# A hybrid linear-attention block on one core: decay weights made in the projection, loaded in the mixing stage, and idle products in TensorE's waits

## The chip, the cores and the metric

One core of a Trainium2 chip runs the whole program. The metric is the device time of one execution in microseconds (us), the median of several. PE is TensorE's matmul stream, DVE is VectorE, ACT is ScalarE, POOL is GpSimd, and SP is SyncE, which here only issues DMAs.

## What is computed

One layer over 1024 latent tokens and 256 context tokens of width 1024, in float32, then a final norm of the latent tokens. Cut to what matters here:

```python
p = h @ w_in                                   # q_a k_a v_a g_a r_a | qkv_b g_b a_b beta_b
# group A: gated linear attention, 4 heads, dk 64, dv 128; both directions
lr = einsum('btr,zrk->zbtk', r_a, w_lr) + b_lr
log_a = log_sigmoid(lr) / 16                   # decay of every key dimension
b = cumsum(log_a within a chunk)
scores = sum_d q[i] k[j] exp(b[i] - b[j])      # j <= i, inside a chunk
dS = (k * exp(b_last - b))^T v                 # state of a chunk
inter = (q * exp(b)) @ S_prev
# group B: gated delta rule, 4 heads, chunk 64: a triangular system is solved per chunk,
# and the state is carried from chunk to chunk; both directions
x = x + gt1 * (concat(norm(o_a)*silu(g_a), norm(o_b)*silu(g_b)) @ w_out)
x = x + gt2 * (relu(norm(x) @ w1)**2 @ w2)
```

## The kernel before

The program has five phases, each a block of instruction streams, one stream per engine, with semaphores between them: `modulate_phase` (norm and modulation), `project_phase` (the product with `w_in`), `mix_phase` (both attention groups), `merge_phase` (output product) and `mlp_phase`. The order on each engine is written out by hand, and an engine never overtakes a waiting instruction.

**Projection.** Products are made with split operands (high and low part, three matmuls for each), over 15 units of at most 256 columns of `w_in`. Each unit is turned into outputs, which are listed in order in `outs`; the outputs go round robin through three PSUM buffers `ps_main`, so that PE may start output i once ACT has copied output i-3. The last units are `ka`, `qa` (keys and queries of group A), two `va` units with 10 tiles of 128 tokens each, and four `gate` units with 8 tiles each. ACT copies every tile (L817), makes the high part of the next unit's weights at the first output of a unit (`split`, L713), and DVE makes the low part (L849). In the gate units, PE also makes 32 groups of late modulation columns, one behind each tile: it loads 512 KB of `w_ada` for each (SP, L585, four buffers), multiplies (`late_columns`, L981), DVE copies the row (`late_out`, L894), and PE turns the row of the tile before (`late_turn`, L987), for which DVE's copy must be there. The low-rank decay of group A (10 outputs `lr`, one for each token tile) is made among the k and v units: a matmul, then on ACT a copy, Abs, Exp and Ln (L755 and L783 to L787), and one operation on DVE (L947); POOL stores it as the scratch tensor `la`.

**Mixing.** Ten steps: two for the context tiles, then eight for the latent tiles. Step p prepares tile p (PE: `system`, `turn_system`, six `level`s, that double the size of the solved blocks) and carries the delta-rule state over tile r = p-1 (`solve`, `update`, `answer`, `predict`, `query`). Between two levels DVE merges a result into `zz` (`factor`, L1538) and ACT copies its transpose (`keep_turned`, L1415); PE's next level waits for both. Group A's work lies between these: PE sums the decays (`cumulate`, L1800), ACT copies the sums (L1433, L1435) and takes the chunk's rates, DVE makes differences for the keys (`differ_keys`, L1579) and for six levels of block size (`differ_level`, L1588 and L1590, two operations each), ACT takes their exponentials (L1449, L1454, L1445), and POOL multiplies them with keys and queries (L1344, L1349, L1356). PE then makes `scores` in two groups (levels 0 to 2 and 3 to 5), turns the keys, and makes the chunk states and the outputs. The steps 0 to 2 have idle products already (`keep_busy`, L1863), products with the unit matrix whose result nobody reads: 34, 34 and 22 of them.

In ACT's stream of a step, what stands between the copies for level 2 and level 3 is `delta(r, 1)` ahead and then this:

```python
keep_turned(p, 2)
if lat(p):
    decay_level(p, 3)
if p + 1 < NT:
    decay(p + 1)          # 8 Abs and one Exp on the next tile's rows
keep_turned(p, 3)
```

Of the kernel before, what the change touches and what calls it, by code (L numbers as in the profile page):

```python
# [21 lines left out]
ALU = mybir.AluOpType  # L22
# [427 lines left out]
def project_phase(nc, A, K, S):  # L450

    with ExitStack() as ctx:
# [11 lines left out]
        NU = len(UNITS)  # L464
        raw = m.sb("raw", [P, 2, KT, W])
        whi = m.sb("whi", [P, 2, KT, W], F32R)
        wlo = m.sb("wlo", [P, 2, KT, W], F32R)
        u_sb = m.sb("u_sb", [P, NTOK])
        y_sb = m.sb("y_sb", [P, NTOK])
        z_sb = m.sb("z_sb", [P, 2, NTOK])  # L470
        sq_sb = m.sb("sq_sb", [P, NTOK])
        n_sb = m.sb("n_sb", [P, 2, NTOK])
        tok_sb = m.sb("tok_sb", [P, 2, NT, P])
        a_sb = m.sb("a_sb", [P, NTOK])
# [6 lines left out]
        lr_x = m.sb("lr_x", [P, 2, 512])  # L481
# [17 lines left out]
        st_tok, st_a = [m.sem("st_tok0"), m.sem("st_tok1")], m.sem("st_a")  # L499
# [4 lines left out]
        st_lr = [m.sem("st_lr0"), m.sem("st_lr1")]  # L504
# [4 lines left out]
        arow = u_sb[:, :2 * P].rearrange("p (x n) -> p x n", n=P)  # L509
        late = [z_sb[:, 0, :KT * P], z_sb[:, 1, :KT * P], n_sb[:, 0, :KT * P], n_sb[:, 1, :KT * P]]  # L510
        ld_a = [m.sem(f"ld_a{i}") for i in range(4)]
# [5 lines left out]
        VA = [un[0] for un in UNITS].index("va")  # L517
        LAST_GATE = NU - 1
        sum_m = lr_x[:].rearrange("p a n -> p (a n)")[:, :6 * P].rearrange("p (x d n) -> p x d n", x=3, d=2)
        rowt = lr_e[:80, :3 * P]  # L520
# [3 lines left out]
        for u, (kind, _, width, h0) in enumerate(UNITS):  # L524
# [3 lines left out]
            elif kind in ("k", "v", "q", "ka", "qa"):  # L528
                for j in range(2):
                    for s in range(2 if kind in ("q", "qa") else 3):  # L530
                        outs.append((u, kind, j, s))
                        n_lr = sum(o[1] == "lr" for o in outs)
                        if n_lr < NT:
                            outs.append((u, "lr", n_lr, 0))
            else:
                for t in range(TL if kind == "gate" else NT):
                    outs.append((u, kind, t, 0))

# [19 lines left out]

        block = ctx.enter_context(nc.Block())
# [7 lines left out]
        def _(sp):  # L567
# [9 lines left out]
            def load_late(g):  # L577
                if g < 2:
                    sp.wait_ge(n_done, 8)
                elif g < 4:  # L580
                    sp.wait_ge(st_n[g - 2], 4 * 16 + 2 * 16)
                else:
                    sp.wait_ge(ar_ready, g - 3)
                c0 = LATE0 + g * P
                sp.dma_start(late[g % 4].rearrange("p (k n) -> p k n", n=P), av[:, :, c0:c0 + P]).then_inc(ld_a[g % 4], 16)  # L585
# [7 lines left out]
            def load_sums():  # L593
                for b in range(2):
                    sp.wait_ge(st_lr[b], 80)
# [2534 lines left out]
```

## Time and profile before

| | us |
|---|---|
| median of 3 runs | 1661.21 |
| lowest and highest | 1659.8, 1670.68 |
| the profiled execution | 1662.78 |
| its span, first to last instruction | 1661.0 |
| PE busy in the span | 1515.7 (91%) |
| DVE busy | 942.2 (57%) |
| ACT busy | 738.9 (44%) |
| POOL busy | 367.4 (22%) |

The profile is of one execution. A span is the time between the first and the last instruction, and the execution is 1.8 us longer. The modulation lasts until about 62 us, the projection until 506 us, the mixing from 508 to 874 us, the output product until about 1005 us, and the MLP until the end.

### The profile page before, as it was taken

What the parts mean: (1) busy time and instruction counts of PE and PEld (TensorE: products, weight loads), DVE (VectorE), ACT (ScalarE), POOL (GpSimd) and SP (SyncE); (2) the same over time, 40 slices, a digit from 0 to 9 for tenths busy, and PEclk for the clock granted to TensorE, in tenths of its full rate; (3) what the DMA queues carried; (4) which work ended last, traced back from release to release, by engine and by line L of the source; (5) the groups of instructions that cost most, each with busy time, mean ns of one, the idle gap of its engine ahead of it and who ended that gap; (6) DMA issues with size and microseconds to landing.
All of it is one profiled execution on the core that took longest, in us unless ns stands there. A gap on an engine that the chain in (4) does not pass through costs nothing. (4 is left out here: it accounts for less than half of the span.)

```text
span 1661.0 us, 34354 instructions
## 1 busy us (share of the span) xinstructions
PE 1515.7 (91%) x14584; PEld 1283.4 (77%) x14584; DVE 942.2 (57%) x1310; ACT 738.9 (44%) x1303; POOL 367.4 (22%) x315
## 2 busy tenths in 40 slices
PE   7699999999996878777778997899999999999997
PEld 6477887899996867766667886788888878888885
DVE  4344553111101487787777439455555598988875
ACT  6477336211114545565544225455555554333333
POOL 0002111111101255565543105232222200000000
PEclk9699999999998999899999999999999999999999
DMA  9313424245554444544414311244444586454322
GB/s 326 87 58 105 130 83 120 84 151 156 172 162 132 130 129 132 153 134 130 123 35 155 125 64 64 95 140 140 159 157 161 174 319 253 142 186 158 122 89 101
DMA packets 179657, 229.94 MB, mean 138 GB/s; under 512 B 34253, under 2 KB 112465, under 8 KB 179506
## 3 DMA queue, kind: packets, MB, share of 16 engines
q1 hardware_dynamic: 172994, 206.91, 38.8%
q0 software_dynamic: 6512, 20.84, 4.0%
q8 instruction: 116, 1.90, 0.5%
q14 instruction: 35, 0.29, 0.1%
HBM read 165.98 MB, written 61.73 MB: 137 GB/s over the span
## 5 line engine op out<-in xcount | busy, mean ns | idle before, releaser
L87 PE MATMUL fps<-xh_m,w1r_hi 128*128 128x512 f32 x448 | 175.9, 393 | 9.5 <-ACT s L2563 2.9
L89 PE MATMUL fps<-xh_m,w1r_lo 128*128 128x512 f32 x448 | 175.2, 391 | 0.0
L87 PE MATMUL fps<-bh,ah 128*128 128x512 f32 x448 | 174.5, 390 | 0.6 <-DVE acc L2892 0.6
L88 PE MATMUL fps<-xl_m,w1r_hi 128*128 128x512 f32 x448 | 175.0, 391 | 0.0
L89 PE MATMUL fps<-bh,al 128*128 128x512 f32 x448 | 174.4, 389 | 0.0
L88 PE MATMUL fps<-bl,ah 128*128 128x512 f32 x448 | 174.4, 389 | 0.0
L80 PE MATMUL ps_main<-hhi,whi 128*128 128x512 f32 (+1 forms) x336 | 126.6, 377 | 0.0
L2535 ACT ACTIVATE ah<-araw 128x2048 fp32r<-128x2048 f32 x28 | 53.7, 1918 | 163.6 <-PE fps L89 134.3
L81 PE MATMUL ps_main<-hlo,whi 128*128 128x512 f32 (+1 forms) x336 | 123.2, 367 | 0.0
L82 PE MATMUL ps_main<-hhi,wlo 128*128 128x512 f32 (+1 forms) x336 | 123.1, 366 | 0.0
L80 PE MATMUL ps_main<-whi,hhi 128*128 128x256 f32 x416 | 120.2, 289 | 0.0
L81 PE MATMUL ps_main<-wlo,hhi 128*128 128x256 f32 x416 | 117.6, 283 | 0.0
L82 PE MATMUL ps_main<-whi,hlo 128*128 128x256 f32 x416 | 117.4, 282 | 0.0
L87 PEld LDWEIGHTS fps<-xh_m,w1r_hi 128*128 128x128 f32 x448 | 84.6, 189 | 29.6 <-issue 7.1
L87 PEld LDWEIGHTS fps<-bh,ah 128*128 128x128 f32 x448 | 84.1, 188 | 18.8 <-issue 1.4
L89 PEld LDWEIGHTS fps<-xh_m,w1r_lo 128*128 128x128 f32 x448 | 84.5, 189 | 17.6
L88 PEld LDWEIGHTS fps<-xl_m,w1r_hi 128*128 128x128 f32 x448 | 84.5, 189 | 17.5
L89 PEld LDWEIGHTS fps<-bh,al 128*128 128x128 f32 x448 | 84.1, 188 | 17.6
L88 PEld LDWEIGHTS fps<-bl,ah 128*128 128x128 f32 x448 | 84.1, 188 | 17.2
L2737 DVE TENSOR_TENSOR w1r_lo<-w1raw,w1r_hi 128x512 fp32r<-128x512 f32 x96 | 74.7, 779 | 36.8 <-ACT w1r_hi L2526 36.8
L817 ACT ACTIVATE t_sb<-ps_main 128x256 f32<-128x256 f32 x52 | 19.9, 383 | 149.8 <-PE ps_main L82 149.8
L849 DVE TENSOR_TENSOR wlo<-raw,whi 128x2048 fp32r<-128x2048 f32 x14 | 32.1, 2292 | 89.9 <-ACT whi L713 89.9
(326 smaller groups left out, 3524.8 us busy)
## 6 DMA issues: line engine op xcount, KB each, us to landing
s_hid<-hb SPq DMA_DIRECT2D x112, 256.0 KB, 2.3
araw<-s_hid SPq DMA_DIRECT2D x28, 1024.0 KB, 5.9
w1raw<-in_w_ff SPq DMA_DIRECT2D x16, 1024.0 KB, 6.0
w2b<-in_w_ff SPq DMA_DIRECT2D x16, 1024.0 KB, 9.9
raw<-in_w_in SPq DMA_DIRECT2D x14, 1024.0 KB, 5.5
z_sb<-in_w_ada SPq DMA_DIRECT2D x16, 512.0 KB, 4.4
n_sb<-in_w_ada SPq DMA_DIRECT2D x16, 512.0 KB, 4.6
kc<-s_k SPq DMA_DIRECT2D x20, 256.0 KB, 3.3
```

The costliest lines, as they stand in the source:

```text
L80: pe.matmul(out, lhi, rhi, start=start, stop=False)
L81: pe.matmul(out, lhi, rlo, start=False, stop=False)
L82: return pe.matmul(out, llo, rhi, start=False, stop=stop)
L87: pe.matmul(out, lhi, rhi, start=start, stop=False, skip_group_check=True)
L88: pe.matmul(out, lhi, rlo, start=False, stop=False, skip_group_check=True)
L89: return pe.matmul(out, llo, rhi, start=False, stop=stop, skip_group_check=True)
L817: act.activation(t_sb[:, nt % 4], ps_main[:, i % 3, :W], ACT.Silu if kind == "gate" else ACT.Copy).then_inc(main_out, 1)
L849: dve.tensor_tensor(wlo[:, u % 2, :, :w], raw[:, u % 2, :, :w], whi[:, u % 2, :, :w].bitcast(F32), ALU.subtract).then_inc(lo_done, 1)
L2535: act.activation(flat(a_hi[v][:]), flat(araw[n % 2][:]), ACT.Copy).then_inc(a_hi_done, 1)
L2737: dve.tensor_tensor(w1r_lo[:, i], weight(n), w1r_hi[:, i].bitcast(F32), ALU.subtract).then_inc(w_lo, 1)
```

## The change

The exponentials of group A's decay leave the mixing stage. The projection makes them, weighs keys and queries with them, and stores the finished tensors (`kin` for the chunk states, `qin` for the outputs between chunks, `wl` for the six levels, `gqk` for keys and queries). The mixing stage loads them.

In the projection: `lr` is made with the key dimension on the partitions, 12 outputs instead of 10 (8 of 512 tokens and 4 of 256), and these stand among the outputs of `qa`, of the first four `va` tiles and of the last four. DVE writes each with two operations and sums it with scans (`decay_sums`: 16, 8 and 16 scans of 130 elements). Then 17 items follow, each 128x2048 elements (one has half that): DVE makes differences (`weight_sums`), ACT exponentials (`weight_exp`), DVE multiplies (`weigh`), SP stores 1 MB. There are two slots for items; an item's differences wait for the store of the item two before. Items 0 to 8 go with the 20 `va` tiles, one for each two tiles, items 9 to 16 with the first 16 gate tiles. The late modulation columns have three buffers instead of four, and their first loads wait for the eighth item.

In the mixing stage: `cumulate`, `differ_*`, `decay_queries/keys/level` and `weigh_level/keys/queries` go, and SP loads `kin`, `gqk`, and `wl` in two halves. A latent step gets thirteen idle products: five in front of `predict(r, 1)`, five in front of level 3, three behind level 4; in the third step, which has `keep_busy` already, only the last three.

```diff
@@ project_phase
+        ITEMS = [(0, kind) for kind in KINDS] + [(2, KIN)] + [(1, kind) for kind in KINDS]
+        starts = [1 + 2 * i for i in range(9)] + [20 + 2 * i for i in range(8)]
+        SUMS_AT = {place(n): i for i, n in enumerate(starts)}
+        WEIGH_AT = {place(n + 1): i for i, n in enumerate(starts)}
@@ sync
             def load_late(g):
-                if g < 2:
-                    sp.wait_ge(n_done, 8)
-                elif g < 4:
-                    sp.wait_ge(st_n[g - 2], 4 * 16 + 2 * 16)
+                if g < NL:
+                    sp.wait_ge(wt_done, 8 if g < 2 else 9)
+                    sp.wait_ge(st_qk, 16)
                 else:
-                    sp.wait_ge(ar_ready, g - 3)
+                    sp.wait_ge(ar_ready, g - NL + 1)
...
+            def store_item(i):
+                t0, n, kind, w, _, _ = item(i)
+                sp.wait_ge(wt_done, i + 1)
...
+                for z in range(2):
+                    sp.dma_start(dst[:, :, z].rearrange("t p a n -> p t (a n)"), w[:, z]).then_inc(st_w[i % 2], 16)
...
+            for g in range(NL, NLATE):
                 load_late(g)
+                if g % 2 == 0 and 9 <= 7 + g // 2 < len(ITEMS):
+                    store_item(7 + g // 2)
@@ scalar
+            def weight_exp(i):
+                t0, n, kind, w, cs, nc_ = item(i)
+                log_exp()
+                act.wait_ge(df_done, i + 1)
+                if kind < KIN:
+                    act.activation(w, w, ACT.Exp, scale=GLA_DECAY).then_inc(ex_done, 1)
+                    return
...
+                    if (u, j) == (VA + 1, 4):
+                        chunk_rates(0)
+                        chunk_rates(2)
+                    if (u, j) == (VA + 2, 0):
+                        chunk_rates(1)
+                    if (u, j) in SUMS_AT:
+                        weight_exp(SUMS_AT[(u, j)])
@@ vector
+            def decay_sums(part):
...
+                dve.wait_ge(lr_done, (4, 12, 8)[part])
+                for x in range(4 * PART[part][1]):
+                    at = slice(2 * PW * x, 2 * PW * (x + 1))
+                    last = dve.tensor_tensor_scan(cs[:, at], restart[:], cs[:, at], 0.0, ALU.mult, ALU.add)
+                last.then_inc(cs_done, 1)
+            def weight_sums(i):
+                t0, n, kind, w, cs, nc_ = item(i)
+                if i >= 2:
+                    dve.wait_ge(st_w[i % 2], 32 * (i // 2))
...
+                dve.tensor_tensor(view(w, 0, out_), view(cs, z + h, edge), view(cs, z, span), ALU.subtract)
+                dve.tensor_tensor(view(w, h, out_), view(cs, h + 1, span), view(cs, h, edge), ALU.subtract)
+                dve.tensor_tensor(view(w, k, out_), view(cs, h, edge), view(cs, 1, span), ALU.subtract)
+                dve.tensor_tensor(view(w, k + h, out_), view(cs, z + h, span), view(cs, z + h, edge),
+                                  ALU.subtract).then_inc(df_done, 1)
+            def weigh(i):
+                t0, n, kind, w, _, _ = item(i)
+                dve.wait_ge(ex_done, i + 1)
...
+                dve.tensor_tensor(w, w, by, ALU.mult).then_inc(wt_done, 1)
...
+                if (u, j) in WEIGH_AT and kind != "lr":
+                    weigh(WEIGH_AT[(u, j)])
+                if (u, j) in SUMS_AT and kind != "lr":
+                    weight_sums(SUMS_AT[(u, j)])
                 if kind == "gate":
                     late_out((u - NU + 4) * TL + j)
@@ mix_phase, sync
             def linear(s):
-                after(sp, kin_done, s)
+                after(sp, kt_ready, s)
+                sp.dma_start(kin[:], S["kin"][s]).then_inc(ld_kin, 16)
                 if lat(s):
...
+                    sp.dma_start(gqk[:], S["gqk"][n]).then_inc(ld_qk, 16)
+                    sp.dma_start(wl[:, 0:3], S["wl"][n, :, 0:3]).then_inc(ld_wl[0], 16)
+                    after(sp, sc_ready, 2 * n)
+                    sp.dma_start(wl[:, 3:6], S["wl"][n, :, 3:6]).then_inc(ld_wl[1], 16)
@@ mix_phase, tensor
+            def idle_states(s, n):
+                pe.wait_ge(gs_out[1], s)
+                for _ in range(n):
+                    pe.matmul(pg[:, 0, :P], K.ident[:], K.ident[:], start=True, stop=True)
+            def idle_solves(s, n):
+                for d in R2:
+                    pe.wait_ge(st_done[d], 2 * s)
+                for _ in range(n):
+                    pe.matmul(pr[1][:, :P], K.ident[:], K.ident[:], start=True, stop=True)
...
-                    cumulate(p)
                     system(p)
...
                     turn_system(p)
                     if p <= TC:
                         keep_busy(p, 4)
+                    else:
+                        idle_states(p, 5)
                 if r is not None:
                     predict(r, 1)
...
                         scores(p, 0)
                     if p <= TC:
                         keep_busy(p, 6)
+                    else:
+                        idle_solves(p, 5)
                     level(p, 3)
...
                     level(p, 4)
                     if p < TC:
                         keep_busy(p, 6)
+                    else:
+                        idle_solves(p, 3)
                     turn_keys(p)
```

## Rows read from the trace of the kernel before

**Rows 1.** Windows of 40 us: PE, PEld, DVE, ACT, POOL busy; PEclk, DMA share, GB/s
```profile
400.00:440.00 40.00, 40.00 (x444) 36.36 (x444) 5.44 (x12) 6.01 (x12) 5.69 (x11) 1.00 0.66 198
...
680.00:720.00 40.00, 31.37 (x907) 28.28 (x898) 30.22 (x63) 23.89 (x66) 22.80 (x18) 0.91 0.45 132
```

**Rows 2.** Waits of PE, 500 to 880 us: total us, times, longest
```profile
PE pd L1734 <- ACT gdn_gt L1415: 30.8, 13, 4.3
PE pr L1748 <- DVE st L1566: 16.4, 9, 2.0
```

**Rows 3.** Timeline of PE, one latent step: start us, us, group [idle before]
```profile
721.66 1.16 PE L1800 MATMUL pg<-tri,gla 128*128 128x128 f32 x8
...
729.90 1.09 PE L1748 MATMUL pr<-st,kc 128*64 128x128 f32 x16 [2.02 <-DVE st L1566]
...
743.55 1.14 PE L1734 MATMUL pd<-gdn_zz,gdn_gt 64*64 64x64 f32 x32 [4.31 <-ACT gdn_gt L1415]
...
745.47 1.71 PE L1748 MATMUL pr<-st,kc 128*64 128x128 f32 x16
...
749.65 0.93 PE L1834 MATMUL pg<-wl 64*64 64x64 f32 x48 [0.73 <-ACT kin L1458]
...
756.07 1.16 PE L1800 MATMUL pg<-tri,gla 128*128 128x128 f32 x8
```

**Rows 4.** Timeline of PE: starts of steps 3 and 9, counted from 0
```profile
614.38 1.16 PE L1800 MATMUL pg<-tri,gla 128*128 128x128 f32 x8
...
829.02 1.16 PE L1800 MATMUL pg<-tri,gla 128*128 128x128 f32 x8
```

**Rows 5.** Timeline of DVE in the latent step before, 686 to 722 us
```profile
689.89 2.32 DVE L1579 TENSOR_TENSOR kin<-bs 128x512 f32<-128x512 f32 x1
...
692.80 1.27 DVE L1566 TENSOR_TENSOR st<-st,pr 128x512 f32<-128x512 f32 x2
...
698.07 0.42 DVE L1590 TENSOR_TENSOR wl<-bs 128x256 f32<-128x256 f32 x1
...
703.77 1.49 DVE L1590 TENSOR_TENSOR wl<-bs 128x256 f32<-128x256 f32 x1
705.18 0.76 DVE L1538 COPY_PREDICATED gdn_zz<-lev_m,pd 128x256 f32<-128x256 uint32 x2
...
713.67 1.11 DVE L1559 SCALAR_TENSOR_TENSOR rr<-pr,gt,vtn 128x128 f32<-128x128 f32 x4
```

**Rows 6.** Timeline of ACT in the same step
```profile
705.29 0.63 ACT L1454 ACTIVATE wl<-wl 128x512 f32<-128x512 f32 x1 [3.10 <-DVE wl L1590]
705.83 2.00 ACT L1393 ACTIVATE ebc<-ebc,gt 128x64 f32<-128x64 f32 x8
...
708.40 0.64 ACT L1415 ACTIVATE gdn_gt<-pd 128x256 f32<-128x256 f32 x2
```

**Rows 7.** Timeline of PE in a context step: eight matrix instructions of four idle products
```profile
554.73 1.16 PE L1863 MATMUL po<-ident 128*128 128x128 f32 x8
```

**Rows 8.** Timeline of ACT in the projection, `va` and gate tiles
```profile
327.40 0.38 ACT L817 ACTIVATE t_sb<-ps_main 128x256 f32<-128x256 f32 x1 [3.61 <-PE ps_main L82]
327.68 1.90 ACT L713 ACTIVATE whi<-raw 128x2048 fp32r<-128x2048 f32 x1
330.28 0.38 ACT L817 ACTIVATE t_sb<-ps_main 128x256 f32<-128x256 f32 x1 [0.70 <-PE ps_main L82]
...
382.84 1.28 ACT L817 ACT_TABLE_LOAD   x1
```

**Rows 9.** Timeline of DVE in the gate tiles
```profile
387.53 2.29 DVE L849 TENSOR_TENSOR wlo<-raw,whi 128x2048 fp32r<-128x2048 f32 x1 [1.32 <-ACT whi L713]
...
393.40 0.29 DVE L894 COPY u_sb<-ps_sq 128x128 f32<-128x128 f32 x1 [3.38 <-PE ps_sq L981]
397.26 0.29 DVE L894 COPY u_sb<-ps_sq 128x128 f32<-128x128 f32 x1 [3.56 <-PE ps_sq L981]
```

**Rows 10.** Timeline of PE in the k units: the matmul of one `lr` output
```profile
121.93 1.12 PE L1060 MATMUL ps_main<-wlr,raT 17*128 17x512 f32 x2
```

More of the change, by code:

```diff
@@ L508, in project_phase @@
         NLATE = (NADA - LATE0) // P
-        arow = u_sb[:, :2 * P].rearrange("p (x n) -> p x n", n=P)
-        late = [z_sb[:, 0, :KT * P], z_sb[:, 1, :KT * P], n_sb[:, 0, :KT * P], n_sb[:, 1, :KT * P]]
-        ld_a = [m.sem(f"ld_a{i}") for i in range(4)]
+        arow = lr_x[:, :2 * P].rearrange("p (x n) -> p x n", n=P)
+        late = [room[:, x:x + KT * P] for x in (0, KT * P, 4 * KT * P)]
+        NL = len(late)
+        ld_a = [m.sem(f"ld_a{i}") for i in range(NL)]
         ar_ready, ar_out, sel_done = m.sem("ar_ready"), m.sem("ar_out"), m.sem("sel_done")
@@ L557, in project_phase, with place, item, view @@
         TURNS = ((0, 4), (4, 4), (8, 2))
+        PART = ((0, 4), (4, 4), (8, 2))
+        KIN, QIN = LEVELS, LEVELS + 1
+        KINDS = [KIN, QIN] + list(range(LEVELS))
+        ITEMS = [(0, kind) for kind in KINDS] + [(2, KIN)] + [(1, kind) for kind in KINDS]
+        def place(n):
+            if n < 2 * NT:
+                return VA + n // NT, n % NT
+            return VA + 2 + (n - 2 * NT) // TL, (n - 2 * NT) % TL
+        starts = [1 + 2 * i for i in range(9)] + [20 + 2 * i for i in range(8)]
+        SUMS_AT = {place(n): i for i, n in enumerate(starts)}
+        WEIGH_AT = {place(n + 1): i for i, n in enumerate(starts)}
+        def item(i):
+            part, kind = ITEMS[i]
+            t0, n = PART[part]
+            return t0, n, kind, slots[i % 2][:, :512 * n], (cs_ctx if part == 2 else cs_lat), 4 * n
+        def view(t, off, dims):
+            return bass.AP(t.tensor, t.offset + off, [t.ap[0]] + dims)
         block = ctx.enter_context(nc.Block())
@@ L621, in _ @@
                 sp.wait_ge(st_g[i], 32)
+            for i in range(2):
+                sp.wait_ge(st_w[i], 32 * ((len(ITEMS) + 1 - i) // 2))
         @block.gpsimd
@@ L1791, in answer @@
                     last.then_inc(o_ready, 1)
-            def cumulate(s):
-                pe.wait_ge(ld_la, 16 * (s + 1))
-                pe.wait_ge(ld_tri, 16)
-                after(pe, gs_out[1], s)
-                for z in R2:
-                    for a in R2:
-                        x = 2 * z + a
-                        last = pe.matmul(pg[:, 0, head(x)], gla[:, head(x)], tri[:, z], start=True, stop=True)
-                last.then_inc(b_ready, 1)
             def turn_keys(s):
-                pe.wait_ge(kin_done, s + 1)
+                pe.wait_ge(ld_kin, 16 * (s + 1))
                 after(pe, gs_out[0], s)
@@ L1868, in step @@
                 if p is not None:
-                    cumulate(p)
                     system(p)
```

368 lines of the change are left out of this document (154 added, 214 removed).

## The prediction, made before the changed kernel was run

> **What bounds the kernel now.** I read the windows first, then PE's waits, then the timelines of one latent step and of the projection's tail. In the gate tiles PE is busy for all 40 us of a window, while DVE works for 5.4 and ACT for 6.0 us of it [rows 1]: the projection is bound by PE, and the two others have room. In the mixing stage PE is busy for 31 of 40 us at a mean granted clock of 0.91, and DVE for 30 [rows 1]: there PE waits in its order for the others. The waits say for what: 30.8 us for the ACT copy L1415 and 16.4 us for DVE's state sum L1566 [rows 2]. In one latent step of 34.4 us (756.07 less 721.66) PE waits 2.02 us ahead of `predict(r, 1)` and 4.31 us ahead of level 3, and twice more for less than 0.8 us each [rows 3]. After the long wait the next groups run slower: 1.14 us for level 3's first half, and 1.71 for a group of `predict` that took 1.09 us earlier in the step [rows 3]. Over steps 3 to 8 a step lasts (829.02 - 614.38) / 6 = 35.8 us [rows 4].
>
> What stands behind the two waits is the work that the change takes away. The state sum at 692.80 starts behind DVE's key difference of 2.32 us [rows 5]. Ahead of level 3, DVE makes the differences of level 3 at 1.49 us for an operation that takes 0.42 us when POOL doesn't multiply, and merges `zz` only at 705.18 [rows 5]; ACT takes an exponential at 705.29, then the 2.0 us of Abs and its Exp, and copies at 708.40 [rows 6].
>
> **Mixing stage, a latent step.** I take the step's queues and set them up again without the removed work, with the durations of the rows. PE's own work: 34.4 less the waits (2.0 + 4.3 + 0.7 + 0.8) and less 1.4 lost at the low clock behind the long wait is 25.2; `cumulate` takes 1.1 of it [rows 3], which leaves 24.1. Thirteen idle products add 13 x 0.235 = 3.1 us, since four of them take 0.94 (eight matrix instructions in 1.16 us, of which about 0.2 overlaps the next group) [rows 7].
> - Ahead of `predict(r, 1)`: DVE's state sum no longer queues behind the key difference and ends some 5.6 us into the step, while PE ends `turn_system` at 6.2. The wait of 2.0 is gone, and the five products that stand in it cost 1.2 us in full.
> - Ahead of level 3: DVE can merge as soon as level 2 is out; ACT makes the Abs and Exp of `decay(p + 1)`, 2.6 us, already while PE is at level 2, and copies right behind the merge. The wait of 4.3 falls to 0.6, and five products fill it: they cost 0.6, and the slow 1.4 us are not lost again.
> - Behind level 4: nothing waited there; three products cost 0.7. Ahead of level 4 a wait of 0.5 is new, because DVE sums the first scores in between (late next on DVE). The waits of 0.7 and 0.8 for ACT's copies of PSUM stay.
> - Sum: 24.1 + 3.1 + 0.5 + 0.7 + 0.8 = 29.2; I take 29.5 us for what the rows don't show. The loads move nothing on the path in this sum: SP issues `kin` and `wl` behind `turn_keys` and the scores, over 15 us ahead of their readers; a step adds 1.3 MB net, 45 GB/s to the 132 that fill 0.45 of the DMA engines [rows 1], which makes about 0.70 in the shorter step. Behind them in SP's queue stand the rows, keys and values of the next tile. If all of this were late, a step would keep some 2.5 us more: 32. If the products cost nothing it would be 28.
> - Six steps save 6 x (35.8 - 29.5) = 38. The last latent step has no long wait and saves 2.7. Step 2 keeps its 22 busy products and saves 4, the context steps lose `cumulate` and a wait behind it, 2 to 2.5 each. Together 49 us, between 36 and 58.
>
> **Projection.** PE's own work hardly changes: 5120 columns of `lr` before and after, at 1.1 us for 512 [rows 10]. New is what DVE and ACT do ahead of PE's releases. An item is a serial chain. DVE's differences of a level are four operations of 512 elements: from 0.42 us for 256 and 2.29 us for 2048 elements [rows 5, 9] about 0.6 us each, 2.4. ACT's exponential of 2048 elements 1.9 (as L713 [rows 8]). DVE's product 2.3 (as L849 [rows 9]). With three handovers of 0.1: 6.9 us, and 5.9 for the items of keys and queries. They can't overlap: DVE's order is product i, then differences i+1, and ACT waits in the middle with PE's next copies queued behind. Two `va` tiles take PE 2 x 2.88 = 5.8 us (330.28 less 327.40 [rows 8]); two gate tiles 7.7 (397.26 less 393.40, doubled [rows 9]). So the chain is slower than PE in the `va` units and just fits the gates.
>
> Going tile by tile from the end of the last `qa` product: the first item starts only at 13 us, behind 16 scans, the unit's low part (2.3) and an `lr`. No row shows a scan; a DVE operation of 128 elements takes 1.11 / 4 = 0.28 [rows 5], and I take 0.35 for 130 (between 0.28 and 0.55): 16 take 5.6. The nine items take 56 us, and within the chain fall the `lr` work of ACT (four operations of 0.4 to 0.6 us each, eight times), eight more scans, and two splits. PE's first gate tile ends at 86 us, where it ended at 62. Of these 24 us, 8 are `lr` products that the k and v units no longer have. That leaves 16 us. Then the last 16 scans come right behind the last `lr`: ACT's rates and item 9 wait for them, and `late_out(0)` stands behind item 9 on DVE. PE waits for it in `late_turn(0)`, 6 us, and in `late_turn(1)`, 5 us, since the unit's split and item 9's product come before `late_out(1)`. The same meeting of split and item at the ninth gate tile costs 2.5. Table loads of 1.28 us [rows 8], two for each item in the gates, lie beside DVE's differences. Waits of 5 us leave PE slow behind them, as in the mixing stage: 2. DMA in the gates: 0.66 of the engines at 198 GB/s [rows 1] is 300 GB/s for all of them, so a 1 MB store needs 3.5 us; 0.66 x 7.7 + 3.5 = 8.6 us of engine time falls into 7.7. With three buffers for the late columns this costs between 0 and 7 us in eight pairs; I take 2. Sum: 16 + 11 + 2.5 + 2 + 2 = 33.5 us, between 15 and 55.
>
> The Trainium skill, "DVE: opcode table, instruction layouts, handler registers and perf-mode slots", section 6, says that the built-in scan runs at half throughput. No row here has a scan. By that rule 130 elements, that stream in about 0.14 us by the slope of rows 5 and 9, would take as much again, the 40 scans 5.5 us longer, of which some 4.5 would reach PE: 1650 instead of 1646.
>
> **Sum.** 1662.8 (the profiled execution) - 49 + 33.5 = 1647.3; that execution is 1.6 us above the median, so 1646 for the median, 0.9% below 1661.2.
>
> **Rivals.**
> 1. The stores hold DVE: slower. An item's differences wait for the store of the item two before, and `late_out` and the splits stand behind that wait on DVE. It decides once a store, queued in SP behind a late load or a unit's weights, lands later than about 4.6 us after the product (7.7 + 6.9 - 10 us that lie between). For it: 8.6 us of DMA work in 7.7, and one queue for both. Against it: the DMA engines are free in the `va` units, and two slots give slack. Each of the eight items of the gates would lose the 3.5 us of one store, and PE some 0.7 at the low clock behind such a wait (half of the 1.4 above): 8 x 4.2 = 34, so 1646 + 34 = 1680.
> 2. DVE and ACT keep up: the projection loses 8 us only. For it: both are idle for more than 80% there [rows 1]. Against it: the chain of 6.9 us in 5.8. 1661.2 - 49 + 8 = 1620.
> 3. The mixing step stays at 32 us: loads or the products take the place of the waits. For it: the rows and the transposed keys are issued late in a step already, and now stand behind 1.5 MB. Then 15 us of the gain go: 1661.
> 4. The idle products do not do what they say: they stand in waits that are gone. This is in the forecast already, as 1.2 + 0.6 + 0.7 = 2.5 us of each of seven steps, 17 us; it has no other time, and only a step without them would tell.
>
> **How the numbers follow.** A measurement of this kernel can tell about 1% from no change, so faster means below 1644.6 and slower above 1677.8. The forecast has 0.45, its own range 1632 to 1660, a bit under half of it below 1644.6. Rival 1 has 0.17, rival 2 0.18, rival 3 0.20. Faster: rival 2, and the lower part of the forecast with a mixing step of 28 us or short waits in the projection, 0.26: 0.44. Slower: rival 1 but for its lower edge, and a little of rival 3 with long scans: 0.16. Same: what is left, 0.40. The range 1616 to 1680 leaves out half of rival 1 and the outer third of rival 2, 0.15.
>
> **What would show it.** In the windows of the `va` and gate tiles PE's busy time falls below 40, with waits of PE for ACT's copies of the `va` tiles and for `late_out`; these two waits should sum to 25 to 35 us, and DVE should be busy above 25 of 40 us. The mixing stage should begin some 33 us later than at 508. Its latent steps should be 29 to 30 us apart, the wait for L1415 ahead of level 3 gone, the clock at 1.00 through most of it, and POOL nearly idle. Wrong would be: steps above 31 us, a projection that ends before 520 us or after 560, or PE waiting for `ld_wl` or `ld_kin`.

## The result, and the profile after

The changed kernel takes 1676.3 us in the median of 14 executions (1663.4 to 1683.4), the kernel before beside it 1661.7 (14 executions). The ratio is 1.0075, with a 95% interval of 1.0061 to 1.009: about 12 us slower (the two medians lie 15 apart), inside the predicted range, but slower where faster was forecast, and 30 us above the predicted 1646. The profiled execution took 1670.2 us (span 1668.4), 6 below its median; I compare it with the profiled 1662.8 of before, so the profiles show only 7 us of the loss.

Three marks divide the program: the last copy of a gate tile (projection's end), the first issue of `kc<-s_k` (mixing's start) and ACT's table load ahead of the output product (mixing's end).

| us | before | after | difference |
|---|---|---|---|
| last gate copy | 504.5 | 533.6 | +29.1 (predicted +33.5) |
| mixing, start to end | 508.4 to 874.0 = 365.6 | 537.3 to 881.4 = 344.1 | -21.5 (predicted -49) |
| rest of the span | 787.0 | 787.0 | 0 |

The first windows answer to [rows 1]. The columns are PE, PEld, DVE, ACT and POOL busy, granted clock, DMA share, GB/s.

```profile
360.00:400.00 40.00, 34.49 (x226) 30.34 (x225) 23.29 (x32) 22.56 (x39) 5.75 (x11) 0.87 0.73 221
400.00:440.00 40.00, 32.48 (x293) 29.64 (x292) 24.38 (x37) 22.51 (x24) 4.15 (x8) 0.83 0.71 222
...
640.00:680.00 40.00, 33.95 (x835) 30.61 (x832) 18.87 (x47) 14.93 (x43) 10.74 (x9) 0.83 0.51 156
680.00:720.00 40.00, 36.31 (x1069) 33.03 (x1071) 22.09 (x55) 18.50 (x55) 13.51 (x11) 1.00 0.63 181
720.00:760.00 40.00, 31.20 (x938) 28.03 (x934) 19.96 (x49) 18.86 (x56) 12.79 (x10) 1.00 0.68 198
```

In the gates PE now idles 7.5 of 40 us, at a mean clock of 0.83. In the mixing stage DVE fell from 30.2 to 22.1 us and POOL from 22.8 to 13.5, as meant; but PE is busy for only 31.2 us of the last window. Apart from one wait for DVE at the start of the stage (8.4 us, until 551) it hardly waits for the two, as PE's waits from 535 to 900 us show (total, times, longest):

```profile
PE pg L1834 <- issue: 10.0, 11, 2.3
PE pd L1733 <- DVE gdn_gt L1565: 8.4, 1, 8.4
PE pg L1856 <- ACT ga_st L1518: 6.1, 8, 0.8
PE pd L1749 <- issue: 5.4, 3, 3.2
PE pd L1745 <- ACT gdn_gt L1498: 3.4, 7, 1.1
...
PE po L1771 <- issue: 2.8, 1, 2.8
PE pd L1745 <- issue: 2.7, 4, 1.4
```

The 30.8 and 16.4 us of [rows 2] are gone: ACT's copy ahead of a level now costs 3.4 us in all, the state sum nothing. In their place stand waits for "issue", for nothing that the profile shows. PE's timeline shows where they fall:

```profile
722.57 0.56 PE L1745 MATMUL pd<-gdn_zz,gdn_gt 64*64 64x64 f32 x21
724.51 0.39 PE L1745 MATMUL pd<-gdn_zz,gdn_gt 64*64 64x64 f32 x10 [1.38 <-issue]
...
727.90 0.60 PE L1874 MATMUL pr<-ident 128*128 128x128 f32 x3
730.49 0.49 PE L1874 MATMUL pr<-ident 128*128 128x128 f32 x3 [2.00 <-issue]
...
828.61 0.37 PE L1749 MATMUL pd<-gdn_gt,gdn_zz 64*64 64x64 f32 x2 [3.15 <-issue]
```

They stand in the middle of a group of like products, even in the middle of idle products that depend on nothing. No semaphore can explain that. So I numbered PE's instructions in the trace by their start (products, weight loads and PE's 640 instructions that only wait), 30,032 of them, and set them beside the packets of the DMA queue that the profile calls "instruction": 117 packets, 1.92 MB, 16,384 bytes each. 1.92 MB over 30,032 instructions is 64 bytes each, so a packet is 256 instructions. From 600 to 870 us PE has eleven gaps above 0.8 us, and all eleven lie at a number that is 193 modulo 256: at the first instruction of such a block. Five successive blocks, worked out from the trace (us):

```
PE enters the    packet of this   its first      idle
block before     block starts     instruction    ahead of it
719.70           721.94           724.51         1.38
724.51           728.10           730.49         2.00
730.49           734.65           736.84         1.26
736.84           739.17           743.25         0
743.25           743.22           748.20         0
```

A block's packet starts only once PE works on the block before it, between 0 and 5.5 us after its entry, and its first instruction runs at the earliest 2.2 us after the packet's start. If PE is through with the block before by then, it stands. From 540 to 870 us the gaps at block borders sum to 4.1 us in the kernel before and to 22.6 us after. I call them code gaps. Of the 11 waits ahead of `scores` (L1834) three are code gaps; the other eight, 0.73 us each, lie anywhere in a block. The kernel before has eight of 0.73 us there too, four of them under the name of ACT's copy [rows 3], so they are something else.

The latent steps, by the first product of `solve(r, 0)`:

```profile
672.47 1.94 PE L1783 MATMUL pr<-rr,gdn_tt 64*64 64x128 f32 x16
...
703.28 1.07 PE L1783 MATMUL pr<-rr,gdn_tt 64*64 64x128 f32 x16
...
738.98 1.07 PE L1783 MATMUL pr<-rr,gdn_tt 64*64 64x128 f32 x16
...
770.90 1.07 PE L1783 MATMUL pr<-rr,gdn_tt 64*64 64x128 f32 x16
```

They lie 30.8, 35.7 and 31.9 us apart, 33.3 on average over seven steps from 634.9 to 868.0, where [rows 4] gave 35.8 and I forecast 29.5. The group at 672.47 took 1.94 us instead of 1.07: behind a code gap of 2.8 us at 666 PE was at the low clock (0.50 from 666 to 673 us).

### The profile page after: what moved, and what is told of

Same layout as the page of the kernel before. It is cut to its first block and busy times, and to the rows that moved or that the text cites. A ratio compares the mean times of both kernels' runs of the same rounds, so it can differ in the third digit from the quotient of the medians.

```text
span 1668.4 us, 34384 instructions
## 1 busy us (share of the span) xinstructions
PE 1536.9 (92%) x14696; PEld 1303.1 (78%) x14696; DVE 945.7 (57%) x1330; ACT 744.8 (45%) x1249; POOL 271.0 (16%) x237
## 3 DMA queue, kind: packets, MB, share of 16 engines
q8 instruction: 117, 1.92, 0.5%
## 5 line engine op out<-in xcount | busy, mean ns | idle before, releaser
L80 PE MATMUL ps_main<-whi,hhi 128*128 128x256 f32 x416 | 127.0, 305 | 6.7 <-ACT t_sb L879 4.2
L81 PE MATMUL ps_main<-wlo,hhi 128*128 128x256 f32 x416 | 123.3, 296 | 0.0
L82 PE MATMUL ps_main<-whi,hlo 128*128 128x256 f32 x416 | 123.2, 296 | 0.0
L87 PEld LDWEIGHTS fps<-xh_m,w1r_hi 128*128 128x128 f32 x448 | 84.5, 189 | 29.6 <-issue 7.4
L80 PEld LDWEIGHTS ps_main<-whi,hhi 128*128 128x128 f32 x416 | 85.2, 205 | 11.8 <-issue 11.8
L82 PEld LDWEIGHTS ps_main<-whi,hlo 128*128 128x128 f32 x416 | 85.5, 205 | 0.0
```

The lines of the kernel that those rows point to most:

```text
L80: pe.matmul(out, lhi, rhi, start=start, stop=False)
L81: pe.matmul(out, lhi, rlo, start=False, stop=False)
L82: return pe.matmul(out, llo, rhi, start=False, stop=stop)
L87: pe.matmul(out, lhi, rhi, start=start, stop=False, skip_group_check=True)
```

## The experiments

Fourteen kernels. "Code gaps" are the sums from 540 to 870 us. Ratios are to the kernel before; mixing is measured by the marks above.

| run | ratio, 95% | last gate copy | mixing | code gaps |
|---|---|---|---|---|
| before | 1 | 504.5 | 365.6 | 4.1 |
| after | 1.0075, 1.0061 to 1.009 | 533.6 | 344.1 | 22.6 |
| e1_no_idle | 1.0001, 0.9973 to 1.0028 | 535.1 | 337.4 | 27.8 |
| e2_wl_once | 1.0077, 1.0047 to 1.0108 | 538.2 | 338.8 | 20.7 |
| e3_halves | 1.006, 1.0032 to 1.0088 | 528.3 | 346.1 | 22.5 |
| e4_before_idle | 1.0005, 0.9985 to 1.0025 | 504.5 | 363.2 | 10.8 |
| e5_no_store | 1.0052, 1.0029 to 1.0075 | 533.2 | 347.6 | 25.9 |
| e6_no_items | 0.9956, 0.9931 to 0.9981 | 517.8 | 341.2 | 24.9 |
| e7_thin | 0.99, 0.9884 to 0.9916 | 534.5 | 318.3 | 6.5 |
| e8_halves_no_idle | 0.9966, 0.9946 to 0.9986 | 531.9 | 331.4 | 24.0 |
| e9_thin_keys | 0.9985, 0.9962 to 1.0009 | 535.5 | 332.7 | 15.8 |
| e10_late_first | 0.9934, 0.9907 to 0.9962 | 529.9 | 334.7 | 26.4 |
| e11_one_place | 0.9968, 0.9941 to 0.9995 | 535.8 | 332.6 | 23.5 |
| e12_paced | 1.047, 1.0443 to 1.0497 | 529.8 | 417.0 | 7.4 |
| e13_before_thin | 0.9994, 0.9975 to 1.0014 | 503.7 | 364.7 | 0 |
| e14_thin_no_idle | 0.9794, 0.9763 to 0.9825 | 535.6 | 298.5 | 6.0 |

Six of these kernels have the projection exactly as changed (after, e1, e2, e7, e9, e14); its end lies at 533.6 to 538.2 there, so one profile tells that mark to about 4 us only. Mixing spreads as much: with the same products and bytes the stage takes 344.1, 346.1 and 347.6 us in after, e3 and e5, and 337.4, 331.4 and 334.7 us in e1, e8 and e10. Differences of 5 us between two single profiles are not clear of that.

**Who holds up PE's code?** First the new loads of the weights alone:

```diff
+                    if n == 0:
-                    sp.dma_start(wl[:, 0:3], ...).then_inc(ld_wl[0], 16)
+                        sp.dma_start(wl[:, 0:3], ...).then_inc(ld_wl[0], 16)
```

and likewise for `wl[:, 3:6]`.

> The changed kernel with the six levels' weights loaded for the first latent step only; later steps take the same ones, so their scores are not the reference's. Theory A, the loads of 1.5 MB in a step hold up the fetches of PE's code: the waits for nothing (in this trace 24 us of PE's waits between 535 and 900 us) fall to the 7 us that the kernel before has, latent steps come to 29.5 us each, and the kernel is about 20 us faster than the changed one, ratio to the kernel before 0.995. Theory B, the loads are innocent: gaps and steps of 33.3 us on average stay, ratio 1.007.

Measured: code gaps of 20.7 us, mixing 5 us shorter, ratio unchanged (1.0077 against 1.0075). Theory A, my first, falls in this form: taking away the weights' 1.5 MB alone gives nothing that can be told from the spread. Then all loads of the stage, by their size:

```diff
+            def thin(s, c=None):
+                if c is None:
+                    return slice(0, 4 if s >= 4 else P)
+                return slice(c * C, c * C + (4 if s >= 4 else C))
-                    sp.dma_start(kc[b][:, d], S["k"][pos(d, s)]).then_inc(ld_kc[b], 16)
+                    sp.dma_start(kc[b][T, d], S["k"][pos(d, s)][T]).then_inc(ld_kc[b], 16)
...
```

> The changed kernel with all loads of the mixing stage but the output weights' cut to four partitions (or four of each half) from the third latent tile's on, so 1/32 or 1/16 of the bytes; the rest of each tile keeps older values, so the result is not the reference's. In the traces so far every wait of PE for nothing of more than 0.8 us falls on a multiple of 256 of PE's own instructions (offset 193), where the next 16 KB of its code begin; the packet starts on average 2.1 us after PE has entered the block before, and 1.8 us or less where the DMA engines are idle. Theory A, the packets start late because the engines are busy with loads: the mean delay falls below 1 us, the waits at block borders from 22.6 us to under 6, a latent step comes to 29.5 us and the kernel is 20 us faster than the changed one, ratio 0.995. Theory B, the fetch is late by itself (one block ahead, PE faster than it): delay and waits stay above 1.6 and 15 us, ratio 1.004 or more.

Theory A, and further than it said in the ratio (0.990, not 0.995). The kernel is 1.7% faster than the changed one, code gaps fall to 6.5 us, and the mixing stage lasts 318.3 us, 47.3 less than before. Windows and two `solve` groups, five steps apart, of this run:

```profile
640.00:680.00 40.00, 37.98 (x1098) 34.69 (x1098) 23.97 (x59) 17.87 (x53) 15.29 (x12) 1.00 0.20 58
680.00:720.00 40.00, 37.18 (x1166) 33.63 (x1159) 24.07 (x61) 23.36 (x70) 12.76 (x10) 1.00 0.08 25
720.00:760.00 40.00, 37.11 (x1013) 33.63 (x1009) 25.08 (x60) 18.25 (x51) 14.63 (x11) 1.00 0.13 37
```

```profile
665.21 1.07 PE L1790 MATMUL pr<-rr,gdn_tt 64*64 64x128 f32 x16
...
812.97 1.07 PE L1790 MATMUL pr<-rr,gdn_tt 64*64 64x128 f32 x16
```

A step is (812.97 - 665.21) / 5 = 29.6 us, and the clock is 1.00 in every window from 600 to 840 us, where after has 0.96, 0.83, 1.00, 1.00, 1.00 and 0.91. That makes the sum of the 26 us that mixing gains here: 16 us of code gaps, and by an estimate 1.4 + 5.8 + 3.0 = 10 us of PE's busy time at the low clock (35.6 x 0.04, 33.95 x 0.17, 33.05 x 0.09). The windows of the whole stage, first the changed kernel's, then this one's, give the same:

```profile
537.30:881.40 344.10, 290.60 (x7672) 261.57 (x7673) 167.85 (x413) 147.02 (x421) 96.30 (x78) 0.95 0.54 161
538.20:856.50 318.30, 280.26 (x7672) 252.78 (x7672) 168.01 (x413) 146.44 (x420) 96.22 (x77) 0.98 0.26 74
```

PE is busy for 10.3 us less with the same products and idle for 15.5 us less. DVE, ACT and POOL are busy for the same times within 0.6 us, so it is not their work that the loads slowed. The clock records of the changed kernel, behind the first 20 us of the stage, have the low level in four stretches, from 627.1, 654.4, 664.6 and 828.5 us on, 24 us in all; each begins in a code gap or less than 1.5 us behind one. The thin run has none there.

Two numbers of the expectation missed: the gaps at block borders were to fall under 6 us (6.5), and the mean delay from PE's entry into the block before to the packet's start fell from 2.1 to 1.45 us only, not below 1.

Only the keys, queries, values and token-major keys cut down (the same edit on four of the loads):

> The changed kernel with only the loads of the old kind cut down that come in packets of 2 KB for both directions' keys, queries, values and token-major keys (2 MB of the some 5.8 MB of a latent step; four partitions of each, or of each half, from the third latent tile's on; the result is not the reference's). The row broadcasts and the weights' loads stay. Theory A, what holds up the fetches of PE's code is the bursts of these loads, that the kernel before has too, and the weights' 1.5 MB only share in it (5 us of 26 by the run that loaded them once): waits at the block borders fall from 22.6 to 12 us or less, the mixing stage from 344 to 330 us or less, ratio 1.000 or less. Theory B, it takes all the traffic together, no one part of it matters: mixing stays above 338 us, ratio 1.005.

Code gaps fall by 7 us, mixing by 11, the ratio by 0.009 (15 us). Between the theories: the old loads alone do about half of what all together do (0.0175, 29 us), the weights alone nothing that shows. What the row broadcasts do by themselves was not run. Over eight changed kernels (after, e1 to e3, e5 to e8), from 600 to 870 us, blocks whose packet came over 2.5 us late had some 127 of the 2 KB packets started in the 1.5 us behind PE's entry, blocks under 1.2 us had some 35; for the 256 byte packets of the row broadcasts it is about 4 against 110. That is a correlation only.

Can the loads be kept and the queues short? On e8:

```diff
                 sp.dma_start(kc[b][:, d], ...).then_inc(ld_kc[b], 16)
+                sp.wait_ge(ld_kc[b], 32 * (s // 2 + 1))
```

and the same behind seven other loads.

> The kernel with halves and without idle products, with the mixing stage's loads paced: SP issues the next group only when the one before has landed (values, keys, queries, query decays, token keys, each 512 KB; gqk 256 KB; the weights 768 KB twice). The same bytes, no burst of more than 768 KB in flight. Theory A, fetches of PE's code are held up by what stands in the DMA queues ahead of them, and short queues let them through: the mean delay falls from 2.0 to 1.5 us, the waits at block borders from 24 to under 15, mixing from 331 us to 322, ratio 0.991. Theory B, the share of busy engines decides, not the queue's length: waits of 20 us or more stay. Theory C, the loads come late for their readers, PE waits for keys or weights: ratio above 1.000.

Theory C, far stronger than thought: 1743 us. The loads come late for their readers, steps of 40 us and more. The waits of all engines, 560 to 940 us:

```profile
ACT ktn L1512 <- DMA ktn<-s_kt: 67.4, 8, 9.8
POOL bbc L1451 <- DMA bbc<-s_row: 56.6, 9, 15.1
```

Its code gaps are small, but a PE that waits up to 9.6 us at a time for ACT gives the fetch its time; it says nothing on the queues.

The control, the same cut in the kernel before:

> The kernel before with its mixing loads cut down as in the thin run of the changed kernel (four partitions, or four of each half, from the third latent tile's on; all but the output weights'; the result is not the reference's). Theory A, the loads hold up PE's code only where nothing else holds PE: before, the waits for ACT and DVE leave the fetch its time (4.1 us of waits at block borders), so the same cut gives at most 5 us here, against 26 in the changed kernel: ratio 0.997 to 1.000. Theory B, the cut itself makes everything faster (shorter waits for loads, less traffic at the engines), and what it gave the changed kernel says nothing of its change: 15 us or more here too, ratio 0.991 or less.

Theory A: 0.9994, and the code gaps go from 4.1 us to none. Its DMA share fell from 0.45 to 0.13, and its waits stayed:

```profile
PE pd L1741 <- ACT gdn_gt L1422: 33.9, 11, 4.3
PE pr L1755 <- DVE st L1573: 16.4, 9, 2.0
```

So less traffic is worth at most 4 us (by the interval) to a PE that waits for ACT and DVE, and 26 us to one that doesn't.

**What do the idle products cost?** They were taken out of the changed kernel:

```diff
-                    else:
-                        idle_solves(p, 5)
...
```

> The changed kernel without the thirteen idle products of a latent step (nothing of the result depends on them). Theory A, the waits of PE for nothing that the profile shows (about 20 us over the mixing stage) are fetches of PE's code held up by the loads of the weights: the gaps stay, a latent step loses only the 2.5 us that the products add, and the kernel is about 15 us faster than the changed one, a ratio to the kernel before of 0.999. Theory B, the gaps come from the products themselves (more instructions to fetch): the gaps go too, steps of 28 us, 30 to 40 us faster, ratio 0.985. Theory C, the products keep the clock up and are worth their time: PE's clock in the latent steps falls below 0.95, steps get no shorter, ratio 1.007 or above.

Theory A, whose 0.999 lies in the interval: 12 us faster (1.0075 - 1.0001; 7 to 17 by the two intervals). One sign of theory C came too, the clock below 0.95. A window:

```profile
720.00:760.00 40.00, 32.69 (x945) 29.40 (x944) 21.75 (x55) 18.98 (x56) 12.46 (x10) 0.88 0.66 195
```

The clock falls, and the code gaps are no fewer (27.8 us). So the products do hold the clock (0.88 here, 1.00 with them; 0.91 and 0.95 over the whole stage), but cost more than it gives. Without loads in the way:

> The changed kernel with the thin loads and without the thirteen idle products (not the reference's result). Theory A, the products cost their 2.5 us in each of seven steps also where the fetches are in time: 12 to 17 us under the thin run's 1646, ratio 0.980 to 0.983, steps of 27 to 28 us. Theory B, without loads in the way the clock that they keep is worth as much as they take: within 4 us of the thin run, ratio 0.988 to 0.992.

Theory A, at or just past the edge of its numbers: 17.6 us under the thin run by the ratios (0.99 - 0.9794), two steps of 26.7 us below (742.41 less 689.00, halved) and 27.3 on average over seven, and the clock stays at 1.00 from 640 to 840 us without one of the thirteen. PE's timeline, then a window:

```profile
689.00 1.07 PE L1790 MATMUL pr<-rr,gdn_tt 64*64 64x128 f32 x16
...
715.79 1.07 PE L1790 MATMUL pr<-rr,gdn_tt 64*64 64x128 f32 x16
...
742.41 1.07 PE L1790 MATMUL pr<-rr,gdn_tt 64*64 64x128 f32 x16
```

```profile
720.00:760.00 40.00, 37.03 (x1223) 33.50 (x1223) 26.12 (x63) 21.78 (x67) 17.17 (x14) 1.00 0.10 26
```

In the kernel before, where the waits still are:

> The kernel before, with the thirteen idle products of a latent step added at the same three places and nothing else. Theory A, they cost what they take where PE doesn't wait and fill the waits of 2.0 and 4.3 us where it does, so that PE is fast behind them: 3.1 us of products a step, of which some 2 lie in waits, and 1.4 us of slow groups saved: within 1 us a step, ratio 0.998 to 1.004. Theory B, the clock is what holds a step at 35.8 us: 1.5 us or more a step gained, ratio 0.993 or less. Theory C, they are pure cost: 3 us in each of seven steps, ratio 1.012.

Theory A: 1.0005. 22 us of PE's two waits are filled (to 18.0 and 7.2 us), mixing is 2.4 us shorter in the profile, and the code gaps grow from 4.1 to 10.8 us. It fits that a PE which runs more meets more often a block that isn't there; no run shows that alone.

> The kernel with halves, and of the thirteen idle products of a latent step only the five ahead of level 3. Their cost by this case's traces is 0.6 to 1.2 us a step (seven steps, 4 to 8 us), what they can give back is the clock (0.87 to 0.91 from 720 us on without any, 0.91 to 1.00 with all). Theory A, cost and clock cancel: ratio 0.995 to 0.998, as without any. Theory B, the clock is worth more than these five: 0.994 or less. Theory C, they only cost: 1.000.

0.9968 against 0.9966 without any: theory A, cost and clock cancel.

**What does the projection lose?** In two halves:

```diff
+                    for z in range(2):
+                        act.wait_ge(df_done, parts(i) + z + 1)
+                        wz = w[:, C * nc_ * z:C * nc_ * (z + 1)]
+                        act.activation(wz, wz, ACT.Exp, scale=GLA_DECAY).then_inc(ex_done, 1)
```

DVE signals behind each pair of its four differences, and multiplies in two operations.

> The changed kernel, with an item of a level made in two halves (one direction each): ACT takes the exponential of the first half while DVE makes the differences of the second, and DVE multiplies the first half while ACT works on the second. The arithmetic and its bytes are the same. Theory A, the serial chain of differences, exponential and product (6.7 us for two va tiles of 5.8 us) is what the projection loses: the chain falls to about 5 us, six items of the va units save about 1.5 us each, the last gate tile ends 8 to 12 us earlier than at 533.6 us. Theory B, the loss lies with the stores and the late columns' three buffers: the projection's end stays within 2 us of 533.6.

In the changed kernel DVE's item in the `va` units looks like this; sums, exponential (ACT, 1.92 us) and product follow each other, and items start 6.7 us apart where nothing else comes between:

```profile
347.32 0.68 DVE L1024 TENSOR_TENSOR room<-room 128x512 f32<-128x512 f32 x1
...
349.13 0.68 DVE L1027 TENSOR_TENSOR room<-room 128x512 f32<-128x512 f32 x1
351.79 2.29 DVE L1038 TENSOR_TENSOR room<-room 128x2048 f32<-128x2048 f32 x1 [1.98 <-ACT room L801]
354.00 0.69 DVE L1024 TENSOR_TENSOR room<-room 128x512 f32<-128x512 f32 x1
```

In halves the wait is gone and they start 4.8 us apart at best:

```profile
350.71 0.67 DVE L1031 TENSOR_TENSOR room<-room 128x512 f32<-128x512 f32 x1
...
354.32 1.22 DVE L1048 TENSOR_TENSOR room<-room 128x1024 f32<-128x1024 f32 x1
355.52 0.69 DVE L1031 TENSOR_TENSOR room<-room 128x512 f32<-128x512 f32 x1
```

But the projection's end moves by 5 us in this profile and by 4 on the mean of four kernels in halves (531.5) against six without (535.4), half of what theory A asked for. The ratios, 1.006 and 1.0075, don't tell the two apart. DVE's timeline shows one reason: an item's differences wait for the store of the item two before, once in the changed kernel's `va` units and for longer in halves (the second line).

```profile
371.93 0.69 DVE L1024 TENSOR_TENSOR room<-room 128x512 f32<-128x512 f32 x1 [2.29 <-DMA s_wl<-room]
373.02 0.69 DVE L1031 TENSOR_TENSOR room<-room 128x512 f32<-128x512 f32 x1 [4.75 <-DMA s_wl<-room]
```

From 310 to 540 us DVE waits 5.8 us for stores in the changed kernel and 12 us in halves: the faster chain meets the stores. Halves without the stores were not run.

The items' stores left out (`return` in `store_item` for the levels):

> The changed kernel without the projection's stores of the six levels' weights (12 MB); the sums, exponentials and products stay, and the mixing stage loads the same number of bytes from the unweighted keys and queries, so its scores are not the reference's. Theory A, the serial chain and the releases behind it cost the projection its 29 us: the last gate tile ends within 4 us of 533.6. Theory B, the DMA traffic of the gates (stores against late columns with three buffers) costs them: it ends before 520. The mixing stage should last as long as before, 344 us.

533.2: theory A. The two ratios, 1.0052 and 1.0075, lie 4 us apart, and their intervals leave at most 8 us to the stores of the levels (the 3.5 us for a `kin` store stay).

All items left out (sums, exponentials, products, stores; the late columns' first loads then wait for the last scans):

> The changed kernel without the 17 items (no differences, exponentials, products and stores of weights); the moved decay products, their work on ACT and DVE and the scans stay. The mixing stage and the output product load the unweighted keys and queries in their place, so the result is not the reference's. Theory A, the items are what the projection loses: the last gate tile ends at 504.5 + 2 to 8 us, 507 to 513. Theory B, the moved decay products with their serial work and the scans are a large part of it: it ends after 517.

517.8, which by the number is theory B, but 9.7 us of it are a wait that this kernel makes itself, since the first late load still starts late:

```profile
396.12 1.08 PE L1112 MATMUL ps_sq<-room,csil 128*32 128x128 f32 x16 [9.71 <-DMA room<-in_w_ada]
```

Without it the end would lie at about 508, theory A. That subtraction is argued, not run.

**Together.** Halves, and no idle products:

> The changed kernel with both of the edits that made it faster: items of the projection in halves, and no idle products in the latent steps. If the two add up: 1676 - 14 (ratio 1.0001 for no idle products) - 3 (1.006 for the halves), ratio 0.9985. If the earlier end of the projection (528.3) is worth its full 5 us: ratio 0.997. If they don't add up, 1.000 or more.

0.9966 [0.9946, 0.9986]: as if the two add up, and with the full 5 us of the halves (0.997). On top of it, the order of DVE in the gate tiles:

```diff
+                if kind == "gate":
+                    late_out((u - NU + 4) * TL + j)
                 if (u, j) in WEIGH_AT and kind != "lr":
                     weigh(WEIGH_AT[(u, j)])
                 if (u, j) in SUMS_AT and kind != "lr":
                     weight_sums(SUMS_AT[(u, j)])
-                if kind == "gate":
-                    late_out((u - NU + 4) * TL + j)
```

> The kernel with halves and without idle products, and in DVE's order of the gate tiles the copy of the late column's row (late_out) ahead of the item's product and differences instead of behind them. Theory A, PE's waits ahead of turning the row (8.1 us there) and the copies held up behind them come from late_out standing behind the item's product: they go, and the projection ends 5 to 8 us earlier than at 531.9. Theory B, the item's chain is then the late one, since DVE now waits for PE's late columns before it takes the product: the end moves by less than 2 us, or back.

PE's waits ahead of turning the row fall from 8.1 to 4.3 us, its wait for a late column's load grows from 2.2 to 4.0; the end comes 2 us earlier, theory B by its number, within what one profile can tell. The interval overlaps e8's, so the order by itself is not shown to help. The ratio is 0.9934 [0.9907, 0.9962]: this kernel computes the same result as both, is 0.7% faster than the kernel before and, by the two ratios, 1.4% faster than the changed one.

## Why the prediction was wrong

**The projection came out near its number, in part by luck:** +29 us in the profile, 29 to 34 over the six kernels with the same projection, against 33.5. An item's parts were priced well (2.5 us of differences, 1.9, 2.3; 6.7 for the 6.9 of the sum). The first gate tile is copied 13.8 us later (399.1 after 385.3) for my 16, and the gates take 15.3 us more for my 17.5. But two of my terms were off in opposite ways. From 62 us to the last gate copy, before and after:

```profile
62.00:504.50 442.50, 440.42 (x3053) 373.57 (x3057) 124.71 (x188) 161.62 (x219) 59.82 (x91) 0.99 0.40 122
62.00:533.60 471.60, 452.31 (x3059) 385.69 (x3060) 209.57 (x314) 215.62 (x272) 49.75 (x78) 0.97 0.47 145
```

PE is idle for 17.2 us more (19.3 against 2.1), where the waits of my sum made 31.5, and busy for 11.9 us more with hardly more work: that is the low clock (8.9 us of it before, 32.6 after, by the clock records; 24 us more at half the clock are 12), for which I had put 2. The waits for ACT's `va` copies (4.2 and 2.6) and for `late_out` (3.9, 1.5 and, at the ninth gate tile, 2.0, for my 11 and 2.5) come to 14.2 us; I had asked for 25 to 35. A late column waited once for its load, 2.1 us, which was the term of 2. Sixteen scans took 5.23 us, 0.33 each for my 0.35. The operations of 128 elements in [rows 5] take 0.28. By the half throughput of the Trainium skill ("DVE: opcode table, instruction layouts, handler registers and perf-mode slots", section 6), which the prediction worked out as 0.14 us more for each, a scan would take 0.42 us from those 0.28, or 0.49 from the 0.35 of the sum; the trace has 0.33, so the 4.5 us set beside the sum were not there.

**The mixing stage failed, in one sentence of its first part's sum:** "The loads move nothing on the path in this sum". I asked of each load whether its reader would wait, and no reader does. But PE's own code comes by DMA too, and the loads hold it up (e7); in what way is open. With the loads nearly gone, a step takes 29.6 us for my 29.5, and the stage saves 47 us for my 49 (6.5 us of code gaps are still in it, so the closeness is partly luck). The waits for ACT and DVE went where I had said that they would; in the kernel before they had given the fetch its time, and once they were gone PE met the next limit: 18.5 us of code gaps more, and the low clock behind them, which I had set to nothing ("the slow 1.4 us are not lost again"). Against the thin run the two make 16 and 10 us, 26 of the 27.5 us missed there. The steps of 33.3 us are what the prediction itself had called wrong (above 31).

The trace of before showed it, and I didn't ask: the queue "instruction" stands on its page, and its mixing stage has four code gaps of 0.5 to 2 us. The bound that I should have put beside the others is a block in some 4.3 to 4.9 us: on average 2.1 us until the packet starts, and 2.2 to 2.8 from there in the gaps. PE at work does a block in 3.4 us (779.47 to 782.87 in the trace after).

The Trainium skill, "Runtime: NRT & Kernel Launch", section "Instruction fetch mechanics", says that code comes in blocks of 16 KiB, 256 instructions, over a DMA queue of the engine's own; the trace agrees, with 16,384 bytes and the 193 modulo 256. It also says that the fetch is hidden because the engine is slower than it. Here it was not: 22.6 us.

**Rivals.** Rival 3 (a mixing step of 32 us because loads or products take the place, 1661) came nearest: 33.3. Its mechanism, loads late for their readers, is not what happened. Rival 1 (stores hold DVE, 1680) ended near the time by chance: its mechanism is there, but small, with 5.8 us of DVE's waits, and e5 gives the levels' stores 4 us, 8 at most. Rival 2 (8 us for the projection) fell. Rival 4 said that the idle products cost 17 us of the forecast: the runs show 12 us among the loads (7 to 17) and 17.6 without them. It was priced right and was in the forecast; the best kernel here has none.

**What stays open.** The median of the changed kernel is 6 us above its profiled execution, where the forecast had it 1.6 below: nearly 8 of the 30 us missed stand in no profile. What decides when a block's packet starts is not settled: thin loads shorten the delay only from 2.1 to 1.45 us, and even with the engines 0.13 busy some packets start over 2.5 us after PE's entry.

## What to carry to other kernels

Removing the waits of an engine that runs many short instructions puts its instruction fetch next in line; count instructions per microsecond against its blocks, and treat all DMA in that stage as traffic that can delay them, also where no reader of it waits. Waits for "issue" in the middle of a group are the sign, and numbering the engine's instructions modulo the block shows whether they lie at its border. Idle products that keep a clock up are worth their time only in waits that still exist: take them out and measure whenever the waits have changed.

## What was not expected

- PE's code arrives in blocks of 256 instructions, one block ahead, and its first instruction runs 2.2 to 2.8 us after the packet's start in every gap above 0.8 us of the changed kernel (2.3 to 2.7 in the thin run's three, up to 3.8 in e1).
- DMA traffic that nobody waits for cost 26 us of a stage of 344, in code gaps and in clock behind them. The same traffic cost the kernel before 1 us in the profile, and 4 at most by the interval of e13.
- Without the thirteen idle products the clock stayed at 1.00 in e14, from 640 to 840 us with PE busy for 34.1 to 37.0 of 40 us and no gap above 1.2 us; in e1, with code gaps of up to 3.7 us, the windows there have 0.87 to 0.95.
- Pacing the loads, each group behind the landing of the one before, to keep queues short, made a stage of 331 us last 417.
- Making the projection's items faster (halves) moved its end by 4 to 5 us only: DVE then waited 12 us for stores instead of 5.8.
